# A ring of six weight slots, another order inside the delta iterations, and silu of z from tanh in a gated DeltaNet kernel

## What is computed

```python
proj = h @ w_in                       # q, k, v (4096 columns), z (2048), beta and a (32)
qkv = causal_short_conv(qkv, conv_w)  # taps along time, then silu
q, k = l2_normalize(q), l2_normalize(k)
o = chunk_gated_delta_rule(q, k, v, g, beta)     # 16 heads: triangular solve, state update
o = rms_norm(o, o_norm) * jax.nn.silu(z)
return o.reshape(b, t, GDN_V_W) @ w_out
```

## Time and profile before

| | us |
|---|---|
| median of 3 runs (1041.1, 1044.58, 1041.1) | 1041.1 |
| profiled execution | 1046.21 |
| its span | 1044.2 |
| PE busy in the span | 971.8 |
| DVE busy, ACT busy | 590.0, 523.9 |

### The profile page before, as it was taken

One profiled execution on the slowest core, in us unless ns is written; L12 is line 12 of the kernel. 1 busy time (PEld: TensorE's weight loads), 2 busy tenths in 40 slices (PEclk: granted clock), 3 DMA queues, 4 the chain that ended last, 5 costly groups with the idle time before them and its releaser, 6 DMA issues.

```text
span 1044.2 us, 14423 instructions
## 1 busy us (share of the span) xinstructions
PE 971.8 (93%) x5405; PEld 807.2 (77%) x5405; DVE 590.0 (57%) x989; ACT 523.9 (50%) x912; POOL 23.1 (2%) x47
## 2 busy tenths in 40 slices
PE   6899998888888999999999899979999899999998
PEld 5788977777777877888888779966667688888876
DVE  4757874656555655555544677255663555554455
ACT  5555555565656445544443566135563644444353
POOL 6000000000000000000000000000000000000000
PEclk9899999999999999999999999977999899999999
DMA  7544412010101546777554645330002356555543
GB/s 236 183 152 144 139 41 68 17 64 18 65 21 63 178 155 207 237 222 240 191 191 151 207 142 161 99 129 0 1 1 81 111 175 197 184 178 182 181 161 121
DMA packets 105753, 138.27 MB, mean 132 GB/s; under 512 B 4569, under 2 KB 76514, under 8 KB 105698
## 3 DMA queue, kind: packets, MB, share of 16 engines
q1 hardware_dynamic: 103200, 130.04, 38.9%
q0 software_dynamic: 2160, 7.36, 2.1%
q10 hardware_dynamic: 338, 0.12, 0.0%
HBM read 136.45 MB, written 1.05 MB: 132 GB/s over the span
## 4 chain that ended last, share of the span: by engine, by line
PE 76%; DVE 10%; ACT 9%; issue 2%; DMA 2%; ACTq 0%; SPq 0%; DVEq 0%
PE ps L469 15%; PE ps L471 14%; PE ps L470 14%; PE ps L448 4%; DVE w_lo L1460 4%; PE ps L453 3%; ACT w_hi L1029 3%; PE ps L454 3%; PE ps L455 3%; PE ps L680 2%; PE ps L941 2%; PE ps L698 2%; PE ps L981 1%; PE ps L905 1%; PE ps L937 1%
## 5 line engine op out<-in xcount | busy, mean ns | idle before, releaser
L1460 DVE TENSOR_TENSOR w_lo<-w_raw,w_hi 128x2048 fp32r<-128x2048 f32 (+2 forms) x117 | 259.6, 2219 | 242.9 <-ACT w_hi L1029 242.8
L1029 ACT ACTIVATE w_hi<-w_raw 128x2048 fp32r<-128x2048 f32 (+2 forms) x117 | 216.9, 1854 | 256.3 <-PE ps L471 155.5
L469 PE MATMUL ps<-w_hi,x_hi 128*128 128x512 f32 x480 | 194.6, 405 | 13.3 <-DVE w_lo L1460 5.0
L471 PE MATMUL ps<-w_hi,x_lo 128*128 128x512 f32 x480 | 188.3, 392 | 0.0
L470 PE MATMUL ps<-w_lo,x_hi 128*128 128x512 f32 x480 | 188.0, 392 | 0.0
L469 PEld LDWEIGHTS ps<-w_hi,x_hi 128*128 128x128 f32 x480 | 90.7, 189 | 36.4 <-DVE w_lo L1460 10.0
L471 PEld LDWEIGHTS ps<-w_hi,x_lo 128*128 128x128 f32 x480 | 90.6, 189 | 19.8
L470 PEld LDWEIGHTS ps<-w_lo,x_hi 128*128 128x128 f32 x480 | 90.9, 189 | 16.7
L453 PE MATMUL ps<-x_hi,w_hi 128*128 128x256 f32 x320 | 93.2, 291 | 4.0 <-DVE w_lo L1460 3.7
L454 PE MATMUL ps<-x_lo,w_hi 128*128 128x256 f32 x320 | 91.7, 287 | 0.0
L455 PE MATMUL ps<-x_hi,w_lo 128*128 128x256 f32 x320 | 91.6, 286 | 0.0
(11 more groups left out here) (308 smaller groups left out, 1491.2 us busy)
## 6 DMA issues: line engine op xcount, KB each, us to landing
w_raw<-in_ffn_w_in SPq DMA_DIRECT2D x88, 512.0 KB, 4.7
w_raw<-in_gdn_w_in SPq DMA_DIRECT2D x48, 512.0 KB, 4.8
w_raw<-in_ffn_w_out SPq DMA_DIRECT2D x40, 512.0 KB, 3.9
w_raw<-in_gdn_w_out SPq DMA_DIRECT2D x16, 512.0 KB, 4.5
w_raw<-in_ple_w_gate SPq DMA_DIRECT2D x16, 512.0 KB, 4.6
w_raw<-in_kv_w SPq DMA_DIRECT2D x12, 512.0 KB, 4.5
qkvT<-in_cmp_w POOLq DMA_DIRECT2D x8, 512.0 KB, 5.4
w_raw<-in_nsa_w_qg SPq DMA_DIRECT2D x8, 512.0 KB, 4.4
```

Source lines behind the costliest of these rows:

```text
L469: mm(o, hi, w_h, start=first and kk == 0, stop=False, skip_group_check=True)
L471: return mm(o, lo, w_h, start=False, stop=end and kk == n - 1, skip_group_check=True)
L1029: A(whi[:, q, 0:n], raw[:, q, 0:n], ACT.Copy).then_inc(S["hi_done"], 1)
L1460: V.tensor_tensor(wlo[:, q, 0:n], raw[:, q, 0:n], whi[:, q, 0:n], ALU.subtract).then_inc(S["lo_done"], 1)
```

## The change

- **Ring.** Stage qkv loads into six slots: two in `w_raw`, four in the first 8192 columns of `gdn`, which the delta iterations use later. Unit u waits for the split of unit u - 6. POOL's small transfers wait for unit 3.
- **Quarters.** All eight quarters m of an iteration's two z units are spread: DVE has m = v in step v for v = 1 to 5, ahead of `update(v,0)`, m = 6 after `y_out(6,1)`, m = 7 after `vn`, and m = 8 (the next iteration's 0) at the end. ACT has m = 1, 2, (3, 4), none, 5, (6, 7) at the end of steps 1 to 6, after `turned(v,1)`, and m = 8 after `o_out(0)`. PE's `z_part` waits quarter by quarter (`zq_lo`), `z_part(6)` goes ahead of `z_products(6,1)`, `z_part(7)` ahead of the products with the state.
- **Decay rows** of iteration j + 1 are computed at the end of iteration j, with their Exp on ACT; `keys(1)` goes behind `decay_cols`; `o_squares(1)` goes from step 1 to the end of its own iteration; the product of q with the decay on DVE goes from step 1 to step 4.
- **silu(z)**: ACT writes tanh(z/2), DVE one product (1 + tanh) * z, which is twice silu(z); the norm's constants carry the half (4/HD, 4 * EPS * HD). One table load (Exp and Tanh together) takes the place of two in iterations 1 to 3.

```diff
@@ -261,6 +264,14 @@
 
             j, n = divmod(head, 4)
             return 2 * j + n if n < 2 else HK + 2 * j + n - 2
+
+        def ring_raw(u):
+
+            s = u % RING
+            return raw[:, s, :] if s < 2 else gdn[:, 2048 * (s - 2):2048 * (s - 1)]
+
+        def ring_count(u):
+            return 32 * (u // RING) + (16 if u % RING == 0 else 32)
 
         block = ctx.enter_context(nc.Block())
 
...
@@ -340,10 +351,12 @@
             first = raw[:, 0, :].rearrange("p (k n) -> p k n", n=UW)
             sp.dma_start(first[:, 0:4, :], source("qkv", 0, 0)[:, 0:4, :]).then_inc(S["w_first"], 16)
             sp.dma_start(first[:, 4:8, :], source("qkv", 0, 0)[:, 4:8, :]).then_inc(landed[0], 16)
-            load("qkv", 0, 1)
-            for u in range(2, 2 * PAIRS["qkv"]):
-                sp.wait_ge(S["lo_done"], u - 1)
-                load("qkv", u // 2, u % 2)
+            for u in range(1, 2 * PAIRS["qkv"]):
+                if u >= RING:
+                    sp.wait_ge(S["lo_done"], u - RING + 1)
+                dst, src = ring_raw(u).rearrange("p (k n) -> p k n", n=UW), source("qkv", u // 2, u % 2)
+                for part in (slice(0, 4), slice(4, 8)):
+                    sp.dma_start(dst[:, part, :], src[:, part, :]).then_inc(ring[u % RING], 16)
 
             def stream(stage):
                 for u in range(2 * PAIRS[stage]):
...
@@ -625,14 +639,23 @@
+            def decay_rows(j, c):
+
+                pe.wait_ge(S["gtri_done"], 2 * j + c + 1)
+                if c == 0 and j >= 2:
+                    pe.wait_ge(S["olo_done"], 2 * j - 2)
+                for n in range(4):
+                    last = mm(bank((0, 4)[c], 4, P)[:, n, :], gtri[:, c, n, :], tri_gt[:, :], start=True, stop=True)
+                last.then_inc(S["dA_ps"], 1)
+
...
                 def keys(c):
-                    pe.wait_ge(S["silu_done"], 10 + 2 * j if j < 2 else 16)
+                    if j < 2 and c == 0:
+                        pe.wait_ge(S["silu_done"], 10 if j == 0 else 16)
                     if j == 0:
                         pe.wait_ge(S["conv_done"], 15)
-                    else:
-                        pe.wait_ge(S["vn_sb"], 2 * j)
+                    elif c == 1:
                         pe.wait_ge(S["o_sb"], 2 * j)
...
@@ -710,14 +730,13 @@
                     if kk == 3:
                         last.then_inc(S["unit_done"], 1)
 
+                if j == 0:
+                    decay_rows(0, 0)
+                    decay_rows(0, 1)
                 keys(0)
-                decay_rows(0)
-                keys(1)
-                decay_rows(1)
-                if j >= 2:
-                    pe.wait_ge(S["olo_done"], 2 * j - 3)
                 decay_cols(0)
                 decay_cols(1)
+                keys(1)
...
@@ -738,6 +757,7 @@
                     z_products(v, 0)
                     y_products(v, 1)
                     turned(v, 1)
+                z_part(6)
                 z_products(LV - 1, 1)
 
                 pe.wait_ge(S["w_upd"], 14 * j + 13)
@@ -750,25 +770,31 @@
                 for n in range(4):
                     last = mm(bank(2, 4, P)[:, n, :], ktok[:, 0, n // 2, :], bv[:, 0, n, :], start=True, stop=True)
                 last.then_inc(S["s_ps"], 1)
-                for n in range(4):
-                    last = mm(bank(1, 4, P)[:, n, :], dQ[:, 0, n, :], vn[:, 0, n, :], start=True, stop=True)
-                last.then_inc(S["o_ps"], 1)
-                z_part(6)
+                z_part(7)
+                pe.wait_ge(S["vn_sb"], 2 * j + 1)
                 pe.wait_ge(S["s_sb"], j + 1)
                 for n in range(4):
                     last = mm(bank(4, 4, P)[:, n, :], qkvT[:, HK + 2 * j + n // 2, P:T], Ss[:, n, :], start=True, stop=True)
                 last.then_inc(S["ks_ps"], 1)
-                z_part(7)
+                for n in range(4):
+                    last = mm(bank(1, 4, P)[:, n, :], dQ[:, 0, n, :], vn[:, 0, n, :], start=True, stop=True)
+                last.then_inc(S["o_ps"], 1)
+                if j < 3:
+                    decay_rows(j + 1, 0)
                 pe.wait_ge(S["r1_sb"], j + 1)
                 pe.wait_ge(S["w_upd"], 14 * j + 14)
                 for n in range(4):
                     last = mm(bank(2, 4, P)[:, n, :], W[:, 1, n, :], bv[:, 1, n, :], start=True, stop=True)
                 last.then_inc(S["u_ps"], 1)
-                pe.wait_ge(S["vn_sb"], 2 * j + 2)
                 pe.wait_ge(S["qdec_sb"], j + 1)
                 for n in range(4):
-                    mm(bank(3, 4, P)[:, n, :], eq[:, n, :], Ss[:, n, :], start=True, stop=False)
-                    last = mm(bank(3, 4, P)[:, n, :], dQ[:, 1, n, :], vn[:, 1, n, :], start=False, stop=True)
+                    mm(bank(3, 4, P)[:, n, :], eq[:, n, :], Ss[:, n, :], start=n == 0, stop=False, skip_group_check=True)
+                if j < 3:
+                    decay_rows(j + 1, 1)
+                pe.wait_ge(S["vn_sb"], 2 * j + 2)
+                for n in range(4):
+                    last = mm(bank(3, 4, P)[:, n, :], dQ[:, 1, n, :], vn[:, 1, n, :], start=False, stop=n == 3,
+                              skip_group_check=True)
                 last.then_inc(S["o_ps"], 1)
 
...
-                    if v == 1 and j:
-                        o_squares(1, j - 1)
-                    if v <= 3:
-                        quarter(U0["z"] + 2 * j + 1, v - 1)
-                    if v == 3:
-                        quarter(U0["z"] + 2 * j + 1, 3)
                     if v == 4 and j:
                         act.wait_ge(S["on_dve"], j)
                         A(ost[:, 1], ost[:, 1], ACT.Sqrt).then_inc(S["on_root"], 1)
+                    for m in ((), (1,), (2,), (3, 4), (), (5,), (6, 7))[v]:
+                        z_quarter(8 * j + m)
...
                 act.wait_ge(S["s_ps"], j + 1)
                 A(Ss, bank(2, 4, P), ACT.Copy).then_inc(S["s_sb"], 1)
-                for part in range(4):
-                    quarter(U0["z"] + 2 * j + 2, part)
-                o_out(0, j)
-                o_squares(0, j)
                 if j == 0:
                     for u in (13, 14, 15):
                         silu_qkv(u)
-                else:
-                    table(ACT.Silu)
+                if j:
+                    table(ACT.Exp)
                 act.wait_ge(S["unit_done"], U0["z"] + 2 * j + 2)
                 for a in range(TT):
-                    A(zs[:, a], bank(6 + a, 4, P), ACT.Silu).then_inc(S["zs_sb"], 1)
+                    A(zs[:, a], bank(6 + a, 4, P), ACT.Tanh, scale=0.5).then_inc(S["zt_sb"], 1)
+                if j == 0:
+                    table(ACT.Exp)
+                o_out(0, j)
+                z_quarter(8 * j + 8)
+                if j < 3:
+                    decay_a(j + 1, 0)
+                o_squares(0, j)
+                if j < 3:
+                    decay_a(j + 1, 1)
+                else:
+                    for part in range(4):
+                        quarter(U0["gout"], part)
                 o_out(1, j)
-                if j < 3:
-                    table(ACT.Exp)
-                else:
-                    o_squares(1, 3)
+                o_squares(1, j)
+
+            def decay_a(j, c):
...
+            def quarter(u, part):
+                q = u % 2
+                if part == 3:
+                    dve.wait_ge(S["hi_done"], u + 1)
+                else:
+                    dve.wait_ge(S["zq_hi"], 3 * (u - U0["z"]) + part + 1)
+                c4 = slice(part * 512, (part + 1) * 512)
+                V.tensor_tensor(wlo[:, q, c4], raw[:, q, c4], whi[:, q, c4],
+                                ALU.subtract).then_inc(S["lo_done" if part == 3 else "zq_lo"], 1)
+
+            def z_quarter(m):
+                if m < 32:
+                    quarter(U0["z"] + m // 4, m % 4)
+            z_quarter(0)
             dve.wait_ge(S["cum_act"], 2)
...
+                def z_gated(a):
+
+                    dve.wait_ge(S["zt_sb"], 2 * j + a + 1)
+                    stt(out=zs[:, a], in0=zs[:, a], scalar=1.0, in1=bank(6 + a, 4, P), op0=ALU.add,
+                        op1=ALU.mult).then_inc(S["zs_sb"], 1)
...
                     if v == 1:
                         values_scaled(1)
                     update(v - 1, 1)
-                    if v == 1:
+                    if v < 6:
+                        z_quarter(8 * j + v)
+                    if v in (2, 3) and j < 3:
+                        triangles(j + 1, v - 2)
+                    if v == 3 and j:
+                        o_root(j - 1)
+                    if v == 4:
                         dve.wait_ge(S["eq_ex"], j + 1)
                         e4 = eq.rearrange("p (k r) s -> p k r s", r=2)
                         V.tensor_tensor(e4, over(qkvT[:, 2 * j:2 * j + 2, P:T], 2, 2), e4, ALU.mult).then_inc(S["qdec_sb"], 1)
-                    if v in (2, 3):
-                        quarter(U0["z"] + 2 * j + 1, v - 2)
-                        if j < 3:
```

(26 more changed lines are left out.)

72 lines of the change are left out of this document (36 added, 36 removed).

## The result

The changed kernel takes 1080.8 us (median of 5 runs, 1079.5 to 1086.1), beside 1043.96 for the kernel before (median of 5, 1041.1 to 1046.4). The ratio is 1.037, with a 95% interval of 1.034 to 1.040. The prediction was 1091, with a range of 1062 to 1112.

What follows compares the result with a forecast made beforehand. PE, busy for 93% of the span, was taken to bound the kernel. Ring -6.1, steps net +35.7 and ends -1.9 gave +27.7; with +23 for the clock, added to 1041.1, the forecast was 1091 us, range 1062 to 1112.

Steps and rivals of the forecast that it cites:

- case 1: Delta iterations: PE's new waits are there and the clock falls at about half of them; 1091 us, chance 0.48.
- case 2: Delta iterations: the waits are there, the clock holds or falls three times at most; 1069 us, chance 0.25.
- case 3: Delta iterations: the clock falls at each wait and stays down through steps; 1123 us, up to 1140, chance 0.14.
- rival 4: Delta iterations: waits shorter than reckoned, 1.5 us each instead of 2.2; 1058 us, chance 0.06.
- The fifth: Delta iterations: ACT's quarters are ready before DVE asks, so the kernel is faster; 1021 us, chance 0.05.
- The quarters' waits: Delta iterations: PE waits 16 times for DVE's update, held up behind ACT's late quarter copy; 43.3 us lost.
- Less waiting behind ACT: PE's transposes in the delta iterations: ACT's quarters and squares now run inside the new waits; 7.6 us gained.
- Ends and heads: Passages between delta iterations, first head and last end: short PE waits go, the one for quarter 6 grows; sum -1.9 us.
- The ring: Stage qkv: the third unit's wait of 3.7 us and 2.4 us of slow clock behind it go; 6.1 us gained.
- The small transfers: Stage qkv: POOL's 2 MB start some 8 us later and meet units 4 and 5; charged nothing.
- The sum with the clock held: Whole kernel: -6.1 + 35.7 - 1.9 = +27.7 us, without any cost of clock falls.
- The clock: Delta iterations: the new waits bring the clock down, ten falls at 2.3 us; +23 us, from 0 to 54.

Runs made afterwards that it cites:

- e1: The changed kernel with ACT copying each quarter one step earlier, all else the same; 1033.0 us beside 1042.9 for the kernel before, ratio 0.991.
- e2: The kernel before with the ring of six slots alone; 1041.0 us beside 1042.9 for the kernel before, ratio 0.998.

## Why the prediction was right, and where its sizes were off

**The sign and the mechanism** were right: case 1, the waits are there and the clock falls at about half of them. It fell nine times for 16 waits. The rivals fell: the clock did not hold (case 2), nor did it fall at each wait (case 3), and no wait was as short as rival 4 has it. The fifth, the quarters ready in time, is what e1 made true by hand: 1033 where that rival was put at 1021.

**Two readings** were off. The clock leaves the full level in three places of the earlier trace rows, not two: the third is the fall of the earlier trace rows. And the loop that the Trainium skill tells of ("TensorE: Matmul & The Clock Gate", "HAM oscillation — how this bites in real kernels") waits for transfers, some 3 to 5 us each time. That all 16 waits of 2.05 to 3.34 us would cost doesn't follow from it, and nine did.

**The quarters' waits, predicted 43.3, measured 40.7.** Predicted 2.2, 2.8, 3.0, 3.5 in iterations 1 and 2, measured 2.05, 2.65, 2.79, 3.33. Each is 0.15 to 0.2 too long, iteration 0 and 3 alike. The chain ACT, DVE, `update` was read from single rows of before, and held. `z_part(6)`: predicted 1.8, measured 1.72.

**Less waiting behind ACT, predicted 7.6.** The labelled part is there: ten waits of 9.1 us in all became three of 3.2. The unlabelled tenths can't be told apart from the rest. Before and after:

```profile
PE ps L448 <- ACT scr L1172: 9.1, 10, 1.2
```

```profile
PE ps L462 <- ACT scr L1205: 3.2, 3, 1.1
```

**Ends and heads, predicted -1.9.** PE's labelled waits there come to 12.6 us before and 11.5 after, so -1.1: the 0.57, 0.63 and both 0.78 went nearly everywhere, `z_part(6)` brought 6.9, and the output projection starts behind 1.89 us instead of 0.40.

**The ring, predicted 6.1.** Right against before's profiled execution (e2, the ring alone, reaches the first mark 5.9 us earlier), too large for the median: 2 to 5 us. The 3.7 for the wait held (3.4 with the clock's part taken off); the 2.4 for the slow stretch behind it did not: the clock's part in the timed runs is some 0.8. The step that failed is that one execution's head was taken for every execution's. The prediction saw that this execution lay 5.1 us above the median, and didn't ask where.

**The small transfers, charged at nothing**: right. No trace with the ring has a wait for them.

**The sum with the clock held**, predicted +27.7. Measured: 39.8 - 16.2 = +23.6. Of the 4.1 between them the waits' 2.6 are located and 0.8 of the ends; the rest is not.

**The clock, predicted 23, measured 16.2** in the profiled execution, and some 12 as the mean of the timed ones. This is the term that was mis-sized. Ten falls were near nine. The price of one was not: it was taken from one place of the trace, where two neighbouring units differed by 2.4 us and 6.7 us were at half level. Here a fall lasts 4.2 us on average (37.6 / 9) and costs 1.8. Per us at half level the place gave 2.4 / 6.7 = 0.36, less than the 0.43 measured; it was the length of a fall that was too long.

**The time.** Predicted +50.7 on the median of the first runs, 1041.1. Measured 39.8 between the spans: 4.1 less with the clock held and 6.8 less for the clock make the 10.9 between them. Between the medians the loss is 36.8 us, 13.9 less than predicted. That the time itself missed by 10 only is luck: the sum was added to 1041.1, the median of three runs, where five gave 1043.96.

**By iteration** the prediction said 8 us longer with the clock held and 14 with it falling, for iterations 1 and 2. Measured: 58.96 - 52.20 = 6.8, and 12.7.

## What to carry to other kernels

When two engines hand a piece of work on, the second one's place in its program decides what an unready piece costs: keep a step between producer and consumer, and nothing that can be late ahead of the instruction on which the busiest engine depends. Read such an order per step, as "what is the last thing that must have happened", and price the chain in rows. The clock's part is worked out from the time at half level times what that time cost (0.41 to 0.44 here), not from a number of falls, and over several executions: the profiled one had 14 us more of it here than the others' mean.
